# One core, transformer trunk in three-product matmuls: weight slots exchanged at the stage ends, squares and first inputs moved ahead of roots, modulation pieces put in front of each tile

## The reference

```
for l in range(DEPTH):                       # DEPTH = 2, SEQ = 512, D_MODEL = 1024, D_FF = 2816, f32
    mod = (c_act @ w_ada[l] + b_ada[l]).reshape(bsz, 3, 3, D_MODEL)      # shift, scale, gate
    x = modulated_sublayer(x, swiglu_ffn(ffn1...), norm_g[l, 0], norm_g[l, 1], mod[:, 0], 0.5)
    x = modulated_sublayer(x, token_mixing(...),   norm_g[l, 2], norm_g[l, 3], mod[:, 1], 1.0)
    x = modulated_sublayer(x, swiglu_ffn(ffn2...), norm_g[l, 4], norm_g[l, 5], mod[:, 2], 0.5)

def modulated_sublayer(x, fn, g_pre, g_post, m, res_w):
    h = rms_norm(x, g_pre) * (1.0 + scale) + shift
    return x + res_w * gate * rms_norm(fn(h), g_post)
def swiglu_ffn(h, w_in, w_out):
    a, b = jnp.split(h @ w_in, 2, axis=-1)
    return (jax.nn.silu(a) * b) @ w_out
```

## Time and profile before

| what | before |
| --- | --- |
| median of 3 runs | 3120.86 us (3119.76 to 3122.25) |
| profiled execution | 3121.1 us, its span 3119.3 us |
| PE busy | 2929.9 us, 94% of the span |
| DVE busy | 1541.3 us, 49% |
| ACT busy | 1005.0 us, 32% |
| granted TensorE clock, mean over the span | 0.975 |

### The profile page before, as it was taken

One profiled execution on the slowest core, in us unless ns is written; L12 is line 12 of the kernel. 1 busy time (PEld: TensorE's weight loads), 2 busy tenths in 40 slices (PEclk: granted clock), 3 DMA queues, 4 the chain that ended last, 5 costly groups with the idle time before them and its releaser, 6 DMA issues.

```text
span 3119.3 us, 40607 instructions
## 1 busy us (share of the span) xinstructions
PE 2929.9 (94%) x16999; PEld 2558.1 (82%) x16999; DVE 1541.3 (49%) x2236; ACT 1005.0 (32%) x1455; POOL 193.1 (6%) x188
## 2 busy tenths in 40 slices
PE   6999898989999988999989989899899999899998
PEld 5888897777788788889988879877777887888897
DVE  5555236777344446542255552477753554453323
ACT  3322124444422323222242221354443232332212
POOL 1000001221100020000000000021211002000000
PEclk7999999999999999999999999999999999999999
DMA  6555331222112233542226542222111232343321
GB/s 238 176 189 189 109 96 61 61 62 68 41 55 82 81 127 104 189 135 95 97 88 195 186 167 89 88 62 75 51 52 41 68 95 81 109 122 95 102 89 55
DMA packets 358854, 324.53 MB, mean 104 GB/s; under 512 B 12300, under 2 KB 305552, under 8 KB 357776
## 3 DMA queue, kind: packets, MB, share of 16 engines
q1 hardware_dynamic: 357136, 319.77, 32.4%
q10 hardware_dynamic: 1536, 2.16, 0.2%
HBM read 313.43 MB, written 6.29 MB: 102 GB/s over the span
## 4 chain that ended last, share of the span: by engine, by line
PE 85%; DVE 7%; ACT 3%; issue 2%; POOL 0%; ACTq 0%; DVEq 0%; POOLq 0%
PE PS L769 25%; PE PS L771 24%; PE PS L770 24%; PE PS L973 2%; PE PS L786 2%; DVE WL L1573 1%; PE PS L1048 1%; PE PS L1010 1%; PE PS L1070 1%; PE PS L1034 1%; PE PS L1025 1%; PE PS L1022 1%; PE PS L832 1%; ACT WH L1164 1%; PE PS L779 1%
## 5 line engine op out<-in xcount | busy, mean ns | idle before, releaser
L769 PE MATMUL PS<-HH,WH 128*128 128x512 f32 (+1 forms) x2512 | 974.3, 388 | 27.3 <-DVE WL L1562 10.3
L771 PE MATMUL PS<-HH,WL 128*128 128x512 f32 (+1 forms) x2512 | 948.7, 378 | 0.0
L770 PE MATMUL PS<-HL,WH 128*128 128x512 f32 (+1 forms) x2512 | 946.9, 377 | 0.0
L1562 DVE TENSOR_TENSOR WL<-RAW,WH 128x2048 fp32r<-128x2048 f32 x142 | 325.5, 2292 | 515.5 <-ACT WH L1164 515.5
L769 PEld LDWEIGHTS PS<-HH,WH 128*128 128x128 f32 x2512 | 475.7, 189 | 116.7 <-DVE WL L1573 13.7
L771 PEld LDWEIGHTS PS<-HH,WL 128*128 128x128 f32 x2512 | 475.0, 189 | 88.7
L770 PEld LDWEIGHTS PS<-HL,WH 128*128 128x128 f32 x2512 | 476.1, 190 | 82.0 <-issue 2.9
L1164 ACT ACTIVATE WH<-RAW 128x2048 fp32r<-128x2048 f32 x142 | 271.8, 1914 | 792.6 <-PE PS L771 792.6
L769 PE MATMUL PS<-GH,WH 128*128 128x256 f32 x1408 | 405.0, 288 | 18.2 <-DVE WL L1562 17.5
L771 PE MATMUL PS<-GH,WL 128*128 128x256 f32 x1408 | 403.7, 287 | 0.0
L770 PE MATMUL PS<-GL,WH 128*128 128x256 f32 x1408 | 403.3, 286 | 0.0
(11 more groups left out here) (225 smaller groups left out, 3470.3 us busy)
## 6 DMA issues: line engine op xcount, KB each, us to landing
RAW<-in_ffn_w_in SPq DMA_DIRECT2D x176, 512.0 KB, 5.2
RAW<-in_w_in SPq DMA_DIRECT2D x132, 512.0 KB, 4.7
AW<-in_w_ada SPq DMA_DIRECT2D x248, 256.0 KB, 4.8
RAW<-in_ffn_w_out SPq DMA_DIRECT2D x88, 512.0 KB, 4.2
AWB<-in_w_ada SPq DMA_DIRECT2D x5, 2048.0 KB, 16.0
RAW<-in_w_out SPq DMA_DIRECT2D x16, 512.0 KB, 4.0
x_kept<-X SPq DMA_DIRECT2D x2, 2048.0 KB, 7.4
X<-x_kept SPq DMA_DIRECT2D x2, 2048.0 KB, 10.1
```

The costliest lines, as they stand in the source:

```text
L769: pe.matmul(o, ah, bh, start=start, stop=skip, skip_group_check=skip)
L770: pe.matmul(o, ah, bl, start=False, stop=skip, skip_group_check=skip)
L771: return pe.matmul(o, al, bh, start=False, stop=stop or skip, skip_group_check=skip)
L1562: dve.tensor_tensor(wl[:, 0:n], RAW[g % 2][:, 0:n], wh[:, 0:n].bitcast(F32), ALU.subtract).then_inc(w_low, 1)
```

## The change

It touches no load and no arithmetic. Six edits, all in the order of work or in what it waits for:

1. **Weight slots.** `beside(g)` is now true for the last two groups of each `rows_product` (HALVED), not for the first two of the next sublayer. So the former are split into WXH and WXL, as soon as the group three before the last is used, and the latter into WH and WL. Group g+2 of the next sublayer then waits for the slot of group g, which is in use by `first_pair`; before it did not.
2. **Squares.** In ACT's `boundary` the squares of X for the first half come one column pair earlier.
3. **First inputs.** ACT makes the first two input tiles before the root for the second half, not after it; `x_sum` of the second half stands after input tiles 3, 4, 5 and 5 of the first half, not 4 to 7.
4. **Modulation.** DVE makes the four pieces of (i, u) in front of `ffn_tile` (i, u), not behind it. PE makes the sums of chunk i right behind group (i, 1), not behind group (i+1, 1); the chunks' results use two PSUM banks in turn.
5. **First group of a `rows_product`.** Its columns are made in the order banks 6 and 7, 0 and 1, 2 and 3, 4 and 5, and each pair of banks waits for its own release only.
6. **Before the branches' merge.** `low(G_BR)` stands at step 3 of the last item of the mixers, not behind the last tile's copy.

```diff
     def beside(g):
-        return g % NG in (G_MIX, G_MIX + 1, G_FFN2, G_FFN2 + 1) or (g % NG < 2 and now[0] + g // NG > 0)
+        return g % NG in HALVED
     def free(g):
         if beside(g):
-            back = max((e for e in ROW_ENDS if e <= g), default=0) - 3
+            back = min(e for e in ROW_ENDS if e > g) - 4
         else:
             back = g - (4 if beside(g - 2) else 2)
...
-                            if not half and p and (u, i) == (1, 1) and k >= KT // 2:
-                                x_sum(p, 1, k - KT // 2)
+                            if not half and p and (u, i) == (1, 1) and 3 <= k <= 5:
+                                x_sum(p, 1, k - 3)
+                                if k == 5:
+                                    x_sum(p, 1, 3)
...
                     def ada(i):
                         pe.wait_ge(ada_part, at(ada_part, i * KT + (ADA_BEFORE[f] + 2) * KT))
...
-                            if u and i <= n:
-                                ada(i - 1)
-                    if n == FI // 2:
-                        ada(FI // 2 - 1)
+                            if (i, u) == (1, 0):
+                                ada(0)
+                            if u and i < n:
+                                ada(i)
...
-                        for half in (1, 0) if i == 0 else (0, 1):
-                            for j in range(KT):
-                                if i == 0 and bank_free:
+                        for half, j0 in ((1, 4), (0, 0), (0, 4), (1, 0)) if i == 0 else ((0, 0), (0, 4), (1, 0), (1, 4)):
+                            for j in range(j0, j0 + 4):
+                                if i == 0 and j == j0:
                                     bank_free(half, j)
...
+                def merged_free(half, j):
+                    pe.wait_ge(br_mul, at(br_mul, {(1, 4): KT - 2, (0, 0): KT - 1}.get((half, j), KT)))
                 def merged(i):
-                    if i == 0:
-                        pe.wait_ge(br_mul, at(br_mul, KT))
                     pe.wait_ge(m_low, at(m_low, 2 * i + 2))
...
                         for u in range(2):
-                            ffn_tile(f, g0, i, u)
-                            if u == 0 and 1 < i <= n + 1:
-                                ada_columns(f, i - 2)
                             if i < n:
                                 ada_pieces(f, i, u)
+                            ffn_tile(f, g0, i, u)
+                            if u == 0 and 1 <= i <= n:
+                                ada_columns(f, i - 1)
...
+                            if (m, k) == (NM - 1, 3):
+                                low(G_BR)
                             mixers(m, k)
                     take(NM - 1, 1)
-                    low(G_BR)
```

More of the change, by code:

```diff
@@ L829, in ada @@
                         pe.wait_ge(ada_part, at(ada_part, i * KT + (ADA_BEFORE[f] + 2) * KT))
-                        pe.wait_ge(ada_out, at(ada_out, ADA_BEFORE[f] + i))
+                        pe.wait_ge(ada_out, at(ada_out, max(ADA_BEFORE[f] + i - 1, 0)))
                         for q in range(4):
-                            mm = pe.matmul(PS[:, 4, q:q + 1], AACC[i % 2][:, q * P:(q + 1) * P], ones[:, 0:1],
+                            mm = pe.matmul(PS[:, 4 + i % 2, q:q + 1], AACC[i % 2][:, q * P:(q + 1) * P], ones[:, 0:1],
                                            start=True, stop=True)
@@ L841, in ffn_in, with rows_product @@
                             group(u)
-                            if u and i <= n:
-                                ada(i - 1)
-                    if n == FI // 2:
-                        ada(FI // 2 - 1)
-                def rows_product(g0, n, rh, rl, ready, b, bank_free=None):
+                            if (i, u) == (1, 0):
+                                ada(0)
+                            if u and i < n:
+                                ada(i)
+                def rows_product(g0, n, rh, rl, ready, b, bank_free):
                     def column(i, j, half):
-                        wh = WH[(g0 + i) % 2][:, :].rearrange("p (k c) -> p k c", k=2)
-                        wl = WL[(g0 + i) % 2][:, :].rearrange("p (k c) -> p k c", k=2)
+                        wh, wl = (w[:, :].rearrange("p (k c) -> p k c", k=2) for w in halves_of(g0 + i))
                         cols = HALVES[half]
@@ L901, in bank_free @@
                     def bank_free(half, j):
+                        if (half, j) == (1, 4):
+                            pe.wait_ge(x_done, at(x_done, 8 * b))
                         if half and j == 0:
@@ L1148, in _ @@
                     merge()
-                    rows_product(G_WO, 4, lambda k: HH[:, k, :], lambda k: HL[:, k, :], merged, 3 * l + 1)
+                    rows_product(G_WO, 4, lambda k: HH[:, k, :], lambda k: HL[:, k, :], merged, 3 * l + 1, merged_free)
                     ffn_in(3 * l + 2, 1, G_FFN2)
@@ L1241, in boundary @@
                         square_y(b, 1, q)
[L1242 to L1245, removed]
+                        if q < 2 and not last:
+                            square_x(b + 1, 0, 2 * q)
+                            square_x(b + 1, 0, 2 * q + 1)
                     if last:
+                        root_y(b, 1)
                         return
@@ L1249, in boundary @@
                         input_high(b + 1, 0, j)
+                        if j == 1:
+                            root_y(b, 1)
                         if j in (2, 4, 6, 7):
@@ L1584, in ffn_in @@
                         for u in range(2):
-                            ffn_tile(f, g0, i, u)
-                            if u == 0 and 1 < i <= n + 1:
-                                ada_columns(f, i - 2)
                             if i < n:
                                 ada_pieces(f, i, u)
-                    for i in range(min(n, FI // 2 - 2), n):
-                        ada_columns(f, i)
+                            ffn_tile(f, g0, i, u)
+                            if u == 0 and 1 <= i <= n:
+                                ada_columns(f, i - 1)
+                    if n == FI // 2:
+                        ada_columns(f, n - 1)
                 def ffn_tile(f, g0, i, u):
@@ L1619, in ada_columns @@
                     ch = i + ADA_FIRST if f == 0 else i + ADA_ALL - ADA_OWN if i < ADA_OWN else i - ADA_OWN
-                    dve.tensor_copy(MOD[:, 4 * ch:4 * ch + 4], PS[:, 4, 0:4]).then_inc(ada_out, 1)
+                    dve.tensor_copy(MOD[:, 4 * ch:4 * ch + 4], PS[:, 4 + i % 2, 0:4]).then_inc(ada_out, 1)
                 def take(m, i):
```

## The result

| what | before | after |
| --- | --- | --- |
| median of 4 runs each | 3120.31 us (3119.16 to 3122.25) | 3202.01 us (3198.82 to 3208.39) |
| ratio, 95% interval | | 1.0264 [1.0246, 1.0282] |
| profiled execution, span | 3121.1, 3119.3 us | 3199.92, 3198.1 us |
| granted clock, mean | 0.975 | 0.966 |

The changed kernel is 2.6% slower. The predicted time was 3171 us with a range of 3125 to 3223.

What follows compares the result with a forecast made beforehand. PE was taken as the bound, busy for 2929.9 of 3119.3 us. With 157.5 us added and 107.4 taken away, +50 us on 3121.1 gave 3171 us, range 3125 to 3223.

Steps and rivals of the forecast that it cites:

- 21 steady stalls: At PE's chunk sums in later FFN chunks: PE waits 3.1 us for late pieces in each, 65.7 us added.
- first chunks: First two chunks of the four FFNs: DVE's chain starts late; 11.5, 13.4, 16.3 and 13.4 us lost, 54.6 in sum.
- clock behind the 21: Lower PE clock behind the steady chunk-sum stalls: 21 x 1.1 us, 23 us added.
- clock behind four long stalls: Lower PE clock behind the long stalls of the first chunks: 2.5 us each, 10 us added.
- stages outside the FFN inputs: The prediction's terms falling in stages other than the FFN input products: 76.5 us taken away.
- ends of the first FFNs and the rest that falls in the FFN inputs: Remaining terms in the FFN inputs, -26.7 us; the ends of the two first FFNs alone were to give 22.3.
- The clock behind the new stalls: Prediction's section on PE's lower clock behind stalls added by edit 4: 23 plus 10, 33 us in sum.
- The first rival: Every chunk-sum stall brings the lower clock: 29 us more than forecast, 3200 us; chance 0.2.
- The "faster" rival: At the chunk sums, AW does not queue behind RAW, so pieces arrive in time: 3037 us; chance 0.08.
- The start waits: PE's waits at the starts of the last three FFNs, behind the first pair: 5.1, 5.1 and 9 us.
- What was taken away: Gains of edits 1, 2, 3, 5 and 6, at boundaries, first FFNs' ends, merge and w_out: 107.4 us in all.
- the terms for edits 2 and 3: In five boundaries: earlier squares gain 12.1 us, reordered first inputs 16.0 us.

Runs made afterwards that it cites:

- experiment 5: The changed kernel with twelve matmuls of no use before each PE wait for the chunk sums; 3160.59 us, ratio 1.0126.
- experiment 2: The kernel before with only the modulation edit (pieces before each tile, chunk sums one group earlier) put in; 3293.37 us, ratio 1.0556.
- experiment 3: The changed kernel with the AW pieces asked for in front of RAW in SP's list, no longer behind the `low`; 3040.76 us, ratio 0.9743.
- experiment 4: The changed kernel with the AW pieces still asked for only behind the `low`, but issued ahead of the RAW loads; 3063.96 us, ratio 0.982.
- the best version: The kernel of experiment 3, with every FFN also starting as layer 0's first does and LBC's copy ahead of layer 0's last boundary; 3016.25 us, ratio 0.9666.
- experiment 11: The best version with edit 5 (column order and bank releases of a product's first group) undone; 3043.98 us, ratio 0.975.
- experiment 9: The best version with edit 2 undone, so the squares of X come one column pair later again; 3038.89 us, ratio 0.9733.
- experiment 6: The changed kernel with PE's chunk sums back at their old place, DVE's pieces staying in front of each tile; 3116.75 us, ratio 0.9988.

## Why the prediction was right in its sign and low in its size

| term | predicted | measured | from |
| --- | --- | --- | --- |
| 21 steady stalls | 65.7 | 70.3 | 3.35 us each, not 3.1 |
| first chunks | 54.6 | 57.3 | waits 48.8; 8.5 of slow running that the chain covered |
| clock behind the 21 | 23 | 47.6 | 95.1 us at 0.50 |
| clock behind four long stalls | 10 | 10.3 | 20.6 us at 0.50 |
| stages outside the FFN inputs | -76.5 | -83.0 | stage times; the prediction's terms that fall there |
| ends of the first FFNs and the rest that falls in the FFN inputs | -26.7 | -24.8 | by difference: 160.7 less the first four rows (185.5) |

**The step that failed** is the first half of the sum in "The clock behind the new stalls": 21 x 1.1. The 1.1 us was the mean loss behind thirteen scattered stops of about this length in the kernel before, seven of which cost nothing. In the changed kernel 20 of 21 cost about 1.7 or 3.4 us, 2.3 in the mean of all 21. That is +24.6 us of the 31 that were missing, and experiment 5 shows from the other side what the clock is worth. The first rival had the right rule (every stall brings the lower clock), with the chance of 0.2 only. The Trainium skill, page "TensorE: Matmul & The Clock Gate", section "HAM oscillation — how this bites in real kernels", tells of a loop whose waits for data make every round begin slowly; here the trace agrees in 20 rounds of 21, and in all 21 of experiment 2, better than the stops of the kernel before had suggested. What went wrong is the sample: scattered stops were taken to price stops that return in every round. Why the recurring ones fare worse stays open. Length is a rival: seven of the thirteen scattered stops last 2.6 to 2.8 us, the recurring ones nearly all 3.1 or more, and the one that kept the clock is the shortest. But length alone does not decide it. Three of the six scattered stops of 3.2 to 3.3 us kept the clock, the recurring one of 2.60 us in experiment 2 lost it, and so did all five stops of 2.02 us in the boundaries of the kernel before, which the sample left out. Here is the last of them and the window behind it:

```profile
2716.83 0.36 PE L769 MATMUL PS<-HH,WXH 128*128 128x256 f32 x1 [2.02 <-DVE HL L1512]
...
2717.40:2720.70 3.30, 3.30 (x18) 0.50 0.02 5
```

The recurring stops also stand behind other work than the scattered ones, and no run changed only one of these. (A slip of reading beside it: the first of the seven that kept the clock stands at 500.2 us, not at 691.5.)

**The mechanism held.** Stall at the sums, for AACC, for the landing of AW, for its place behind RAW: each link is in the rows above, and experiments 3 and 4 cut two of them separately. The "faster" rival (the pieces are there in time) was wrong for this kernel and right as a mechanism: it named 3037 us, and experiment 3, in which AW is issued first, runs in 3041.

**The first chunks.** The start waits were predicted as 5.1, 5.1 and 9 and stand as 5.17, 5.17 and 9.03. Here is the longest in the timeline of the changed kernel:

```profile
1682.39 0.77 PE L769 MATMUL PS<-HH,WH 128*128 128x512 f32 x1 [9.03 <-DVE SB L1603]
```

The total is 2.7 above what was predicted for all four. In layer 0 the prediction's own times give 130.3 - 118.4 = 11.9 us where it entered 11.5; the stall is 11.87.

**What was taken away** outside the FFN inputs was 6.5 us more than predicted. The stops of 4.4 us on WL are gone, 2.0 us stand at the second input tile (10.1 in five), as foreseen. Undone one by one in the best version, edits 2, 3 and 5 gave 22.6, 21.6 and 27.7 us against 12, 16 and 21. The idle times were about as predicted; part of the rest is lower clock, which the terms for edits 2 and 3 left out or named only as a bound (behind each stop at w_out's start 1.5 us, in experiment 11), and part lies in stages that the edit does not touch, as in experiment 9. How much is the edit's own I did not separate, so these single sizes hold for the best version and not as shares of the change.

**Left over.** The last row of the table is a difference, so the table sums to the measured 78.8 us with the setup's 1.2 by construction. The 1.9 us between that row and its prediction, some 10 of the 38 us of experiment 2 and the 13 of experiment 6 stay open.

## What to carry to other kernels

Before an operand is consumed earlier, read the list of the engine that issues its loads: if the request stands behind a wait on the consumer's own neighbour, the move makes a loop with a period of its own, and two lines in that list were worth more (161 us) than all six edits of the change. Price a stop that returns in every round with the lower clock behind it each time, as 41 of 42 such stops had it in these two kernels, not with the mean of scattered stops. Where such a stop can't be removed, work of no use in it may pay: here it gave 41 us.

## What the runs showed of the hardware that was not expected

- In a regular loop the granted clock fell to 0.50 behind 20 of 21 stops of 2.4 to 4.7 us (changed kernel) and behind 21 of 21 of 2.6 to 4.5 us (edit 4 alone), though about half of the scattered ones of 2.6 to 3.3 us left it at 1.00. Twelve matmuls in each stop held it at 1.00 behind 20 of 21 and gained 41 us.
- Five stops of 2.02 us, one in each boundary of the kernel before but the last, were each followed by 3.4 us at 0.50.
- A transfer of 256 KB landed 5.3 us after its issue behind two of 512 KB on SP's list, and 2.7 us after it ahead of them, in the same place of the program.
